# Order of an expert step on TensorE: gate, activations and next rows turned, last step's down, up

## The reference, cut to what matters

```
lg = (xt @ w_rg + b_rg);  g = argmax(lg)                 # group
top_v, top_i = top_k(le_g, 2);  eid = g * 4 + top_i      # two experts of 16
a = xt @ w1[e];  u = xt @ w3[e]                          # 1024 -> 256 (gate, up)
hdn = silu(a) * u * gate                                 # "hid" in the kernel
y  = hdn @ w2[e]                                         # 256 -> 1024 (down)
x  = LayerNorm(alpha * x + sum of the token's two y)
```

## Time and profile before

| what | us |
|---|---|
| median of 3 runs | 1252.42 (1251.98 to 1254.09) |
| the profiled execution's own time | 1251.31 |
| its span | 1249.5 |
| TensorE busy (matmuls) | 1057.5, 85% of the span |
| VectorE, ScalarE, GpSimd busy | 588.0, 278.0, 292.5 |
| expert steps, first gate product to last down product | 882.87 to 1178.50 |

### The profile page before, as it was taken

How to read it: one execution, slowest core, us unless ns; L and a number is a source line. 1 busy time by engine, 2 the same in 40 slices (tenths; PEclk the granted TensorE clock), 3 DMA queues, 4 the chain that set the end, 5 groups by cost and what they waited for, 6 DMA issues and landing times.

```text
span 1249.5 us, 17577 instructions
## 1 busy us (share of the span) xinstructions
PE 1057.5 (85%) x6776; PEld 632.3 (51%) x6776; DVE 588.0 (47%) x964; ACT 278.0 (22%) x614; POOL 292.5 (23%) x262
## 2 busy tenths in 40 slices
PE   7999999799999679999999988854786899997500
PEld 4666666556565356566666655523443455443200
DVE  0540134457777576977778764385011111111046
ACT  2541121211112222233223311710110111111023
POOL 0000000010111332543345312174100123220175
PEclk9999999899999889999999998855798999999755
DMA  9010101100000700000110032035876785849396
GB/s 385 16 68 0 68 23 45 68 3 2 0 1 1 281 1 1 34 18 18 34 35 17 18 117 95 19 127 210 343 281 277 269 296 201 299 161 349 91 215 183
DMA packets 29286, 145.84 MB, mean 117 GB/s; under 512 B 5498, under 2 KB 5882, under 8 KB 20138
## 3 DMA queue, kind: packets, MB, share of 16 engines
q1 hardware_dynamic: 23546, 121.76, 25.8%
q0 software_dynamic: 5248, 18.94, 5.9%
q10 hardware_dynamic: 432, 4.34, 0.9%
HBM read 313.13 MB, written 23.79 MB: 270 GB/s over the span
## 4 chain that ended last, share of the span: by engine, by line
PE 77%; DVE 8%; DMA 8%; issue 3%; POOL 1%; SPq 1%; ACT 1%; DVEq 0%; ACTq 0%; POOLq 0%
PE psum L1594 17%; PE psum L619 9%; PE psum L602 9%; PE psum L1645 9%; PE psum L1279 5%; PE psum L1284 5%; PE psum L1262 4%; PE psum L638 4%; DMA weight_slots<-in_w_gate 2%; DMA x_cm<-y_slots,hg_k 2%; DMA hg_decay<-in_w_up 2%; PE psum L1247 1%; PE psum L1612 1%; PE psum L704 1%; PE psum L577 1%
## 5 line engine op out<-in xcount | busy, mean ns | idle before, releaser
L1594 PE MATMUL psum<-x_cm,weight_slots 128*128 128x344 f32 x720 | 209.0, 453 | 0.0
L1594 PEld LDWEIGHTS psum<-x_cm,weight_slots 128*128 128x128 f32 x720 | 136.6, 190 | 71.9 <-issue 1.1
L1645 PE MATMUL psum<-weight_slots,x_cm 128*128 128x512 f32 x256 | 113.4, 596 | 0.0
L1279 PE MATMUL psum<-weight_slots,scratch 128*32 128x256 f32 x1280 | 83.5, 419 | 24.1 <-DMA weight_slots<-in_w_gate 13.3
L1517 DVE SCALAR_TENSOR_TENSOR scratch<-scratch,psum 128x256 f32<-128x256 f32 x20 | 9.6, 480 | 165.8 <-PE psum L1284 165.8
L1262 PE MATMUL psum<-conv_qk,scratch 128*32 128x512 f32 x320 | 75.2, 613 | 9.8 <-DMA hg_q<-in_w_down 6.8
L1284 PE MATMUL psum<-conv_qk,scratch 128*32 128x256 f32 x640 | 74.2, 385 | 5.5 <-DMA hg_decay<-in_w_up 5.5
L894 POOL TENSOR_TENSOR scratch<-scratch,hg_k 128x256 f32<-128x256 f32 x56 | 46.0, 821 | 125.9 <-ACT scratch L790 125.9
L1645 PEld LDWEIGHTS psum<-weight_slots,x_cm 128*128 128x128 f32 x256 | 47.8, 192 | 54.1 <-issue 54.1
L1262 PE MATMUL psum<-hg_k,scratch 128*32 128x512 f32 x160 | 75.0, 613 | 0.0
L1262 PE MATMUL psum<-hg_q,scratch 128*32 128x512 f32 x160 | 75.0, 613 | 0.0
(11 more groups left out here) (369 smaller groups left out, 1802.2 us busy)
## 6 DMA issues: line engine op xcount, KB each, us to landing
weight_slots<-in_w_gate SPq DMA_DIRECT2D x80, 1024.0 KB
conv_qk<-in_w_up SPq DMA_DIRECT2D x40, 1024.0 KB
hg_decay<-in_w_up SPq DMA_DIRECT2D x40, 1024.0 KB
conv_qk<-in_w_down SPq DMA_DIRECT2D x40, 1024.0 KB
hg_k<-in_w_down SPq DMA_DIRECT2D x20, 1024.0 KB
hg_q<-in_w_down SPq DMA_DIRECT2D x20, 1024.0 KB
weight_slots<-in_w_in SPq DMA_DIRECT2D x6, 2048.0 KB, 7.7
y_slots<-scratch SPq DMA_DIRECT2D x20, 512.0 KB, 7.2
```

Source lines behind the costliest of these rows:

```text
L1279: m = mm(PS[lane, 2, 0:FF], xgT[i][:, k, lane], w_gate[q][:, k], start=(k == 0), stop=(k == KD - 1))
L1594: i = mm(PS[0:m, idx % 4, 0:PIECE], lhs_of(k), xT[:, k, n * PIECE:(n + 1) * PIECE], start=(k == 0), stop=(k == KD - 1))
L1645: i = mm(PS[:, bank, :], xT[:, k, c * P:(c + 1) * P], w_slot(g)[:, k, :], start=(k == 0), stop=(k == KD - 1))
```

## The change

The diff reorders instructions in the streams of TensorE, VectorE and SyncE. ScalarE and GpSimd keep theirs.

- TensorE: gate(n), turn hid(n-1), turn rows of n+1, down(n-1), up(n). Turning hid gets a function of its own, and the last one stands behind the loop. The wait of gate(n), which was for hid(n-1), is now for silu(n-1).
- VectorE: the copy of the turned hid(n-1), the copy of half of the next rows and of half of y(n-1) come ahead of hid(n) instead of behind it.
- SyncE: in a step, loads of gate(n+1), then down(n) and the store of y(n-1), then up(n+1).

```diff
--- before.py
+++ after.py
@@ -1209,15 +1209,16 @@
                 sp.wait_ge(s.gate_done, pair * 2 + (i + 1))
                 for q, expert, new in coming:
                     load_gate(q, expert, new)
+            if not is_first(pair, i):
+                present = experts_of(n)
+                sp.wait_ge(s.down_done, n)
+                for q, expert, new in present:
+                    load_down(q, expert, new)
+                store_y(*tile_before(pair, i))
+            if not (last and i == 1):
                 sp.wait_ge(s.up_done, pair * 2 + (i + 1))
                 for q, expert, new in coming:
                     load_up(q, expert, new)
-            if not is_first(pair, i):
-                coming = experts_of(n)
-                sp.wait_ge(s.down_done, n)
-                for q, expert, new in coming:
-                    load_down(q, expert, new)
-                store_y(*tile_before(pair, i))
             if isinstance(pair, int) and n == 2:
                 sp.wait_ge(s.outputs, 16 * early_outs[0])
                 keep_x1(4)
@@ -1265,6 +1266,13 @@
         pe.wait_ge(s.state_added, 16)
         turn_x(0, 0)
 
+        def turn_hid(n):
+
+            pe.wait_ge(s.hid_ready, n + 1)
+            for k in range(2):
+                m = nc.tensor.transpose(PS[:, 4, k * P:(k + 1) * P], hid[:, k:FF:2], ident)
+            m.then_inc(s.hid_turned, 1)
+
         def step(pair, i, last):
             n = pair * 2 + i
             pe.wait_ge(s.xgT_ready, n * 2 + 2)
@@ -1273,27 +1281,25 @@
                 pe.wait_ge(s.tiles_known, 1)
                 pe.wait_ge(s.logits_read, NTT)
             else:
-                pe.wait_ge(s.hid_ready, n)
+                pe.wait_ge(s.silu_ready, n)
             for k in range(KD):
                 for q, lane in enumerate(lanes):
                     m = mm(PS[lane, 2, 0:FF], xgT[i][:, k, lane], w_gate[q][:, k], start=(k == 0), stop=(k == KD - 1))
             m.then_inc(s.gate_done, 1)
+            if not is_first(pair, i):
+                turn_hid(pair * 2 + (i - 1))
+            if not (last and i == 1):
+                turn_x(pair + i, 1 - i)
+            if not is_first(pair, i):
+                down(*tile_before(pair, i))
             pe.wait_ge(s.w_up_in, pair * 32 * STREAMS + (i + 1) * 16 * STREAMS)
             for k in range(KD):
                 for q, lane in enumerate(lanes):
                     m = mm(PS[lane, 3, 0:FF], xgT[i][:, k, lane], w_up[q][:, k], start=(k == 0), stop=(k == KD - 1))
             m.then_inc(s.up_done, 1)
-            if not (last and i == 1):
-                turn_x(pair + i, 1 - i)
-
-            if not is_first(pair, i):
-                down(*tile_before(pair, i))
-            pe.wait_ge(s.hid_ready, n + 1)
-            for k in range(2):
-                m = nc.tensor.transpose(PS[:, 4, k * P:(k + 1) * P], hid[:, k:FF:2], ident)
-            m.then_inc(s.hid_turned, 1)
 
         pairs_loop(pe, step)
+        turn_hid(STEPS - 1)
         down(STEPS // 2 - 1, 1)
 
     def scalar_moe(act, link, tell):
@@ -1507,24 +1513,27 @@
 
         x_half(0, 0)
 
+        def copy_hidT(pair, i):
+            dve.wait_ge(s.hid_turned, pair * 2 + (i + 1))
+            if not is_first(pair, i):
+                dve.wait_ge(s.down_done, pair * 2 + i)
+            v.tensor_copy(hidT, PS[:, 4, 0:2 * P].rearrange("p (k t) -> p k t", k=2)).then_inc(s.hidT_ready, 1)
+
         def step(pair, i, last):
             n = pair * 2 + i
+            if not is_first(pair, i):
+                copy_hidT(*tile_before(pair, i))
+            if not (last and i == 1):
+                x_half(pair + i, 1 - i)
+            if not is_first(pair, i):
+                y_half(*tile_before(pair, i))
             dve.wait_ge(s.silu_ready, n + 1)
             dve.wait_ge(s.gate_ready, n + 1)
-            if not is_first(pair, i):
-                dve.wait_ge(s.hid_turned, n)
             dve.wait_ge(s.up_done, n + 1)
             v.scalar_tensor_tensor(hid, silu, gate_c[i], PS[:, 3, 0:FF], ALU.mult, ALU.mult).then_inc(s.hid_ready, 1)
-            if not (last and i == 1):
-                x_half(pair + i, 1 - i)
-            dve.wait_ge(s.hid_turned, n + 1)
-            if not is_first(pair, i):
-                dve.wait_ge(s.down_done, n)
-            v.tensor_copy(hidT, PS[:, 4, 0:2 * P].rearrange("p (k t) -> p k t", k=2)).then_inc(s.hidT_ready, 1)
-            if not is_first(pair, i):
-                y_half(*tile_before(pair, i))
 
         pairs_loop(dve, step)
+        copy_hidT(STEPS // 2 - 1, 1)
         y_half(STEPS // 2 - 1, 1)
```

## The result

The changed kernel takes 1315.72 us (median of 4 runs, 1315.41 to 1319.01) against 1252.2: ratio 1.0515, 95% interval 1.0501 to 1.0530. It is slower, as forecast, but by 63.5 us where 33 were forecast, and outside the range.

What follows compares the result with a forecast made beforehand. TensorE bounds the kernel (77% of the chain). Work 233.1 + moved turn 0.4 + step 1 clock 1.6 + stalls 55.9 + low clock 19.8 + weights 1.0 + last step 3.4 = 315.2 us against 281.89; forecast 1286, range 1262 to 1309.

Steps and rivals of the forecast that it cites:

- The gather's chain: Ahead of turning rows, steps 2 to 18: TensorE waits for a gather released by hid, 17 x 3.29 = 55.9 us.
- L - 2.60: Stall per step ahead of turning rows, L being the gather's time from issue to landing: 1.42 + L - 4.02 us.
- I keep the measured mean: Gathers on GpSimd: mean time from issue to landing stays at the old order's 5.89 us, a stall of 3.29.
- I take nine payments: Products behind the 17 stalls: nine run partly at the low clock, 9 x 2.2 = 19.8 us; bounds 0 and 37.4.
- Step 1's gate: Gate product of step 1: its low clock stays, 5.14 - 3.59 = 1.6 us.
- The price, 2.2: Low clock behind a TensorE wait: 2.2 us each, from 13.4 us paid six times in the kernel before.
- The threshold: Wait length at which TensorE's clock falls: between 2.02 us, which cost nothing, and 3.06 us, which paid in full.
- The rule of the Trainium skill: Rival, all 17 stalled steps start at the low clock: 17 payments instead of nine, +17.6 us, 1303; chance 18%.
- Waits for weights: TensorE's weight waits mostly vanish behind the stalls: 1.0 us left ahead of step 19; bounds 0 and 15.
- The step 1 gather: Gather for step 1's turning of rows: comes in time because that step's gate product was delayed anyway; no stall counted.
- The last step: Step 19 and last down: 0.6 for an unhidden copy plus 2.8 us of remaining wait, 3.4 together, without low clock.
- Moved loads on SyncE at no cost: SyncE sends down loads and the store of y ahead of up loads; nothing stands behind a later wait: no cost.

Runs made afterwards that it cites:

- experiments 9 and 10: Changed kernel without reloads, after the first four experts, of down weights (9: 1290.97 us) or of up weights (10: 1283.45 us), one run each.
- experiments 3 and 4: No weights reloaded after the first four experts, in the changed kernel (3: 1258.74 us) and in the kernel before (4: 1202.40 us), one run each.
- experiment 1: Changed kernel with GpSimd's wait for hid moved behind the gather of rows, so the gather goes a step earlier: 1239.14 us, ratio 0.9897 to the kernel before.
- experiment 5: Changed kernel with SyncE's old order, up loads first, then down loads and the store of y: 1347.92 us, one run.
- experiment 8: Changed kernel with eight matmuls of constants, result unused, ahead of each turning of rows: 1331.08 us, one run.
- experiment 6: Changed kernel with the down product ahead of the turning of rows, and the copies in that order: 1245.11 us, one run.

## Why the prediction was right in kind and wrong in size

- *The gather's chain.* Right: release by hid, 1.42 us to the issue, 4.02 us of products in front. The stall was forecast as L - 2.60; it was L - 2.43 (4.59 against 7.02), 0.17 x 17 = 3 us more.
- *"I keep the measured mean because the load of the up weights starts at the same moment as the gather in both orders (both follow up)."* This step failed. L was 7.02 and not 5.89, 1.13 x 17 = 19 us. I had seen that the down load takes the gate load's place in front of the gather, and counted one against the other. But gate and up loads had met the same gather, and up and down loads meet two different ones (experiments 9 and 10): seven of 17 gathers took 5.6 us or more before, twelve after. Two of the gathers that became slow meet other transfers besides weights of experts, which the prediction did not count. The reload of rows of x (issued at 934.1 and 934.6, the gather at 934.8) and the normalisation weights with the store of states (1206.6 and 1207.0, the gather at 1206.9) now go out right behind the up loads and so beside a gather; before, they went out 5.7 and 5.9 us or more after that gather. These two gathers rose from 5.1 to 9.1 and from 5.4 to 8.7 us, 7 of the 19; without any reload of weights they still take 8.4 and 12.3 in the changed order, and 5.4 and 4.7 in the old one (experiments 3 and 4).
- *"I take nine payments."* Fell with it, and on its own: it was 14 stalls and the last down, 31.2 us against 21.4 with step 1's, 10 us too little. (Step 1's gate, for which 1.6 were kept, paid nothing.) The price, 2.2, was right (31.2 / 15 = 2.1). The threshold was not: stalls of 1.97 and 2.01 paid. The rule of the Trainium skill that I had set beside it ("TensorE: Matmul & The Clock Gate", section "HAM oscillation — how this bites in real kernels": every tile behind a DMA wait starts at the low clock) would have had 17 payments, and 14 are nearer to that than to nine; where the stalls were 2 us long (experiment 3) the trace does not follow it, six of 17 paid.
- *Waits for weights.* Right: none of the big ones is left, 1.0 was allowed for step 19 and 0 came; experiment 1 shows 4.0 and 6.5 us of them again once the stalls are out. The step 1 gather, which I had in time, cost 1.5.
- *The last step.* 3.4 forecast, 0.5 + 0.7 + 2.1 = 3.3 measured.
- *Moved loads on SyncE at no cost.* Right as to their issue, and experiment 5 shows that the old order would have been worse; wrong in that the down load is part of what slowed the gathers (0.83 of 1.91 us in experiment 9).

22 us too little for idle time ahead of turning rows, 10 for the clock and 1.5 in step 1, less 1 for weights, is the 32 between the forecast 315.2 and the 347.6 of the stretch. By these numbers the latency alone would have given 1286 + 19 = 1305 and the clock alone 1296, both inside the range; it took both to leave it. The upper bounds in the working (slowest gathers, all payments) were given, but the range stopped at a mean L of 6.5, though nothing but the traffic of another order stood behind that mean.

## What to carry to other kernels

Before a step is moved up in one engine's order, follow the chain that feeds it across the other engines and ask which event releases it: here one wait on GpSimd, harmless in the old order, turned a gain of 12 us into a loss of 63, and moving that wait behind the gather gives 1239.1 us, the best of all versions. And a latency read from the old trace holds for the traffic of the old order: when transfers change places, list for each which others are in flight, not how many.

## What the runs showed of the hardware

- TensorE fell to its lower level, 1.2 GHz, behind single stalls of 1.97 us in the changed kernel, while stalls of 2.63 us, and 2.94 ahead of step 1's gate, went free; length alone does not decide at that size. The same 2.94 us ahead of the same gate paid in experiment 8 (5.27 us instead of 3.59), and 3.04 ahead of a turning of rows went free in experiment 6. All of 3.52 us and more paid.
- Work that leads to nothing keeps the clock up (0.99 over 373 us), but cost more here than it gave back.
- A gather of 128 rows of 4 KB takes 4.2 to 4.6 us with no weights moving (experiment 3), 7.5 to 9.2 where 2 to 3 MB of other transfers start while it is in flight (changed kernel), and 12.3 beside 1 MB of normalisation weights and a store of 2 MB (experiment 3).
